# A transformer block on one core: attention scores in two passes, with no transposes

## The chip, the cores and the metric

The kernel runs on one core of one Trainium2 chip. The metric is the time of one execution on the device in microseconds (us); lower is better.

## The reference, cut to what matters

The reference is a block of two branches over 1,024 positions of width 1,024, a gated merge, a feed-forward part, a convolution part and a second feed-forward part. The change is in the first branch's attention: 8 heads, 64 + 32 query and key columns, values of 64 columns, no mask.

```python
def blocked_mla_attention(q_nope, q_rope, k_nope, k_rope, v):
    ...
    scale = 1.0 / math.sqrt(QK_NOPE + QK_ROPE)
    ...
        s = (jnp.einsum('bqhd,bkhd->bhqk', qn_b, k_nope)
             + jnp.einsum('bqhd,bkd->bhqk', qr_b, k_rope))
        p = jax.nn.softmax(s.astype(jnp.float32) * scale, axis=-1)
        return jnp.einsum('bhqk,bkhd->bqhd', p.astype(v.dtype), v)
```

The second branch, which shares the stage with attention, is a linear recurrence over the positions with a state of 64x64 for each of 8 heads (`wkv7_scan`), once forward and once backward; the results of both directions are normalized, gated and added.

## The kernel before

The kernel is written in direct mode: each engine has its own instruction stream, and signals (semaphores) with `wait_ge` order them. Positions lie along the free dimension in most stages; weights come in 139 panels of 1 MB, which ScalarE and VectorE split into a high and a low fp32r part, and big products are sums of three fp32r matmuls.

The stage of the change holds the two recurrences and attention. The recurrence is computed in eight steps (tiles of 128 positions) for each direction; these are "ways" d = 0 and d = 1, and way 1 starts 13 places later. One step of a way is cut into named calls: `cum` (prefix sums of the decays, L1335 to L1338, and ScalarE's exponentials of them, L1483 to L1492), `mul` (VectorE's four multiplications L1550 to L1558), `turn` (16 transposes, L1347, and ScalarE's copies L1501 and L1506 into AR, BT and KT), `scores` (L1358, masked by VectorE at L1563), `PV`, `Nc` (a small block to DRAM and back in another layout as Dn, L1696 and L1700), `row0` to `row3` (VectorE's small forward substitution, L1590 and L1592), `spread` (L1598, and three memsets on GpSimd, L1681), `X`, `Y3` to `X5` (the block inverse, L1375 to L1404), `WU` (L1414), `RG` (L1424, added by VectorE at L1627), `OH` (L1432 to L1447), `S0` and `S1` (the state, L1462 and L1468), and `post1` to `post3` (group norm and gate: VectorE L1648 to L1652, a square on ScalarE at L1533, a power on GpSimd at L1684, four multiplications and additions on VectorE at L1660 to L1670).

`slots()` writes one common order for all engines: in each place stands one call of way 1, one call of way 0 and zero, one or two attention halves, by the table `EACH`, which repeats after 27 places and has 16 attention halves in them. Way calls stand first in a place. Every engine runs through this order and takes its part of each call, so an instruction that waits holds up all that stands behind it on its engine.

Attention is cut into 64 units u, each one head h of a pair k and one block of 128 queries. Queries Qb are stationary and keys Kp stream (L1744), so scores lie with queries on the partitions and 1,024 keys along two PSUM banks, 4 and 5. VectorE takes the negated maximum of each row (L1774), ScalarE the exponential with that as its bias and the row's sum in the same instruction (L1790), VectorE the reciprocal (L1777), ScalarE scales the row (L1795). TensorE transposes P in eight blocks of 128x128 into bank 6 (L1767, four in each half), ScalarE copies them to PT (L1785, L1801), and every second unit TensorE multiplies them by the values Vp into bank 7, two heads beside each other on 64 partitions each (L1755). ScalarE copies four such results to Oh (L1807), and GpSimd's queue stores them. Halves c = 0 and c = 1 of unit u are two attention places. A score product waits for the exponential of the unit before.

## Time and profile before

| | us |
|---|---|
| median of 3 runs | 3265.0 |
| lowest and highest | 3261.01 and 3273.98 |
| the profiled execution, own time | 3276.46 |
| its span | 3274.6 |

The profiled execution is one run; its span is the time from its first to its last instruction. Engines are named PE (TensorE's matmuls), PEld (TensorE's weight loads, beside the matmuls), DVE (VectorE), ACT (ScalarE), POOL (GpSimd) and SP (SyncE, whose queue issues most DMAs). An f32 matmul has two records of each kind, an fp32r one has one. Matmuls overlap, so the sum of their durations is more than the time they take: the chain of work counts overlapping records once. L followed by a number is a line of the kernel.

### The profile page before, as it was taken

To read this page: it belongs to the slowest core of one execution; us is meant where nothing else is said; L and a number is where in the kernel's file an instruction comes from. 1 tells how busy PE (TensorE), PEld (TensorE's weight loads), DVE (VectorE), ACT (ScalarE), POOL (GpSimd) and SP (SyncE) were. 2 spreads that over 40 slices of the span, in tenths; PEclk is the share of its full clock that TensorE was granted. 3 is DMA by queue.
4 is the path that set the end of the run, shared out by engine and by line. 5 is a ranking of instruction groups with operands and counts; after the bars stand their busy time and mean duration, and the time that the engine had idled before them with its cause. 6 is when DMAs were issued, how large, how long until landed. Compare 5 with 4: busy or idle time off the path is not lost.

```text
span 3274.6 us, 54823 instructions
## 1 busy us (share of the span) xinstructions
PE 3152.3 (96%) x23414; PEld 2544.0 (78%) x23414; DVE 2012.7 (61%) x3047; ACT 1067.3 (33%) x1528; POOL 374.1 (11%) x354
## 2 busy tenths in 40 slices
PE   8998998899999998999999999999999999999999
PEld 7787886777777777778888888887746888788887
DVE  6665554466766775545444444469979988755544
ACT  5222334445444443222111111132253333433332
POOL 0222441000000000301000000020000000110000
PEclk9999999799999999999999999999999999999999
DMA  3343665122222223421111111111101222223222
GB/s 148 126 135 99 214 213 186 54 75 81 69 86 75 82 81 116 148 90 52 39 52 52 52 42 49 52 39 52 39 13 52 103 91 103 90 90 126 94 91 76
DMA packets 93537, 288.80 MB, mean 88 GB/s; under 512 B 12400, under 2 KB 38640, under 8 KB 72816
## 3 DMA queue, kind: packets, MB, share of 16 engines
q1 hardware_dynamic: 79104, 233.39, 21.1%
q0 software_dynamic: 14192, 51.91, 4.6%
q8 instruction: 186, 3.05, 0.4%
q14 instruction: 55, 0.45, 0.0%
HBM read 228.64 MB, written 56.62 MB: 87 GB/s over the span
## 4 chain that ended last, share of the span: by engine, by line
PE 82%; DVE 10%; ACT 2%; issue 2%; DMA 2%; POOL 1%; SPq 1%; DVEq 0%; ACTq 0%; POOLq 0%
PE ps L2441 24%; PE ps L307 21%; PE ps L489 7%; PE ps L1744 4%; PE ps L2247 3%; PE ps L2603 2%; PE ps L1755 2%; DVE Yh L2630 2%; PE ps L1767 2%; PE ps L2063 1%; PE ps L1387 1%; PE ps L1404 1%; PE ps L1008 1%; PE ps L1398 1%; DVE wlo L287 1%
## 5 line engine op out<-in xcount | busy, mean ns | idle before, releaser
L2441 PE MATMUL ps<-Hh,whi 128*128 128x512 f32 x1600 | 497.6, 392 | 1.3 <-DVE uA L2562 0.7
L283 ACT ACTIVATE whi<-raw 128x2048 fp32r<-128x2048 f32 x139 | 265.5, 1910 | 522.2 <-PE ps L307 296.1
L287 DVE TENSOR_TENSOR wlo<-raw,whi 128x2048 fp32r<-128x2048 f32 x139 | 321.2, 2311 | 95.0 <-ACT whi L283 94.6
L2441 PEld LDWEIGHTS ps<-Hh,whi 128*128 128x128 f32 x1600 | 300.0, 188 | 70.5 <-issue 5.3
L2441 PE MATMUL ps<-Hh,wlo 128*128 128x512 f32 x800 | 311.4, 389 | 0.0
L307 PE MATMUL ps<-Hhi,wlo 128*128 128x512 f32 x672 | 206.9, 389 | 0.0
L307 PE MATMUL ps<-Hlo,whi 128*128 128x512 f32 x672 | 206.9, 389 | 0.0
L307 PE MATMUL ps<-Hhi,whi 128*128 128x512 f32 x672 | 206.8, 389 | 0.0
L2441 PE MATMUL ps<-aHh,whi 128*128 128x512 f32 x512 | 199.5, 390 | 2.7 <-DVE wlo L287 2.5
L2441 PE MATMUL ps<-aLh,whi 128*128 128x512 f32 x512 | 199.2, 389 | 0.0
L2441 PE MATMUL ps<-aHh,wlo 128*128 128x512 f32 x512 | 199.2, 389 | 0.0
L2809 DVE TENSOR_TENSOR xT<-ps,xT 128x512 f32<-128x512 f32 x256 | 169.2, 687 | 21.3 <-PE ps L2441 21.3
L2441 PEld LDWEIGHTS ps<-Hh,wlo 128*128 128x128 f32 x800 | 150.2, 188 | 31.5
L489 PE MATMUL ps<-Hhi,whi 128*128 128x512 f32 (+1 forms) x512 | 163.8, 401 | 0.0
L2309 DVE TENSOR_TENSOR xT<-ps,xT 128x512 f32<-128x512 f32 x176 | 112.3, 686 | 77.0 <-PE ps L307 76.0
L2630 DVE SCALAR_TENSOR_TENSOR Yh<-uB,vc,Yh 128x512 f32<-128x512 f32 x208 | 157.8, 761 | 3.0
L489 PE MATMUL ps<-Hlo,whi 128*128 128x512 f32 (+1 forms) x512 | 158.9, 392 | 0.0
L489 PE MATMUL ps<-Hhi,wlo 128*128 128x512 f32 (+1 forms) x512 | 158.0, 390 | 0.0
L2795 DVE TENSOR_TENSOR aLh<-rth,aHh 128x512 fp32r<-128x512 f32 x64 | 43.5, 722 | 170.2 <-ACT aHh L2789 170.2
L307 PEld LDWEIGHTS ps<-Hhi,wlo 128*128 128x128 f32 x672 | 126.1, 188 | 26.2
L307 PEld LDWEIGHTS ps<-Hhi,whi 128*128 128x128 f32 x672 | 126.1, 188 | 26.2
L307 PEld LDWEIGHTS ps<-Hlo,whi 128*128 128x128 f32 x672 | 126.1, 188 | 26.2
(389 smaller groups left out, 6181.8 us busy)
## 6 DMA issues: line engine op xcount, KB each, us to landing
raw<-in_panels SPq DMA_DIRECT2D x139, 1024.0 KB, 4.8
rwf<-F POOLq DMA_DIRECT2D x16, 1280.0 KB, 6.6
L<-rwf SPq DMA_DIRECT2D x16, 1024.0 KB, 5.0
L<-rwf SPq DMA_DIRECT2D x64, 256.0 KB, 3.5
gts<-so POOLq DMA_DIRECT2D x16, 512.0 KB, 3.5
gl<-gts SPq DMA_DIRECT2D x32, 256.0 KB, 3.6
rwt<-so POOLq DMA_DIRECT2D x15, 512.0 KB, 2.9
qkd<-XTs POOLq DMA_DIRECT2D x16, 384.0 KB, 4.0
```

The source lines that it names most:

```text
L283: e.activation(whi[i % 2][:, :], raw_of(i)[:, :], AF.Copy).then_inc(*a_hi.up(i))
L287: e.tensor_tensor(wlo[i % 2][:, :], raw_of(i)[:, :], whi[i % 2][:, :].bitcast(F32), OP.subtract).then_inc(*v_lo.up(i))
L307: m = e.matmul(aps[h][0:n1 - n0, :], w[wi][:, kc, n0:n1], mov[mi][:, kc, hs(h)], start=x == 0 and q == 0, stop=x == len(kcs) - 1 and q == 2)
L489: m = e.matmul(aps[h][0:n1 - n0, :], W[wi][:, kc, n0:n1], H2[mi][:, kc, hs(h)], start=kc == 0 and q == 0, stop=kc == 7 and q == 2)
L1744: m = e.matmul(bank[4 + half], Qb[g % 3][:, h, :], Kp[k % 2][:, h, hs(half)], start=True, stop=True)
L1755: m = e.matmul(bank[7][64 * n:64 * n + 64, 128 * (w % 4):128 * (w % 4) + 128], Vp[(w // 8) % 2][:, i, 64 * n:64 * n + 64], PT[:, i, n, :], ...
L1767: m = e.transpose(bank[6][:, 128 * q:128 * (q + 1)], Pb[w % 2][:, 128 * i:128 * (i + 1)], ident)
L2247: m = e.matmul(aps[h], W[wi][:, kc, n0:n0 + 128], H2[mi][:, kc, hs(h)], start=kc == 0 and q == 0, stop=kc == 7 and q == 2)
L2309: e.tensor_tensor(xT[:, n, hs(h)], ring.bank("down", p, n, h), xT[:, n, hs(h)], OP.add).then_inc(*v.up("x", b, n, h))
L2441: m = e.matmul(ap, W[wi][:, kc, n0:n0 + 128], mov[mi][:, kc, :], start=x == 0 and q == 0, stop=x == len(kcs) - 1 and q == 2)
L2630: e.scalar_tensor_tensor(out=to, in0=x, scalar=w, in1=to, op0=OP.mult, op1=OP.add).then_inc(*v_e.up(*key))
L2809: e.tensor_tensor(xT[:, n, hs(h)], ring.bank("x", h, b, n), xT[:, n, hs(h)], OP.add).then_inc(*v_e.up("x", h, b, n))
```

## The change

Attention now runs over eight groups g, each a pair of heads and one half (512) of the queries, and over 128 items in place of 128 halves (`att_items`): for each group eight of the first pass ("max") and eight of the second ("exp"). The places in the common order are as before, and four further ones at the end hold what is left.

First pass: as L1744 before, with queries stationary, but read as fp32r, one record per matmul. VectorE takes the negated maxima into negm. TensorE turns the eight columns of a group into rows, by 64 matmuls in all with one stationary column and the identity streaming ("row"), and ScalarE copies them as a 97th partition under the queries Qr. The keys Kr have a 97th partition of ones, set by two memsets at the start.

Second pass: keys are stationary in blocks of 128 and 512 queries of each head stream, in f32 with 97 contraction rows, so the maximum is already subtracted and scores lie with keys on the partitions. ScalarE's exponential of both heads' 512 columns goes to Pe, which is the streaming operand of PV as it stands, accumulated over the eight key blocks in bank 6 or 7. GpSimd adds the eight Pe of a group into acc (seven additions of 128x1024). At a group's end TensorE multiplies acc by a block of ones (L1789, "sum"), which gives every partition of a head the column's sum; ScalarE copies it to Oh (L1856); VectorE takes the reciprocal of 128x512 (L1831) and multiplies PV by it (L1834) ("out"); GpSimd's queue stores it. The recurrences, the places and the rest of the kernel are unchanged.

`ALSO` says behind which item these extra pieces stand. `PAIR` names for each product in banks 4 and 5 the item or sum before it, and `pair_free` waits until that one has been read: a maximum by VectorE, an exponential or a sum by ScalarE.

```diff
-    Kp = [sb(f"Kp{i}", 8 * i, [96, 2, S]) for i in range(2)]
-    Pb = [sb(f"Pb{i}", 16 + 4 * i, [128, S]) for i in range(2)]
-    PT = sb("PT", 24, [128, 8, 2, 128])
+    Kr = [sb(f"Kr{i}", 8 * i, [97, 2, S], F32R) for i in range(2)]
+    Pe = [sb(f"Pe{i}", 16 + 4 * i, [128, 2, 512]) for i in range(2)]
+    acc = sb("acc", 24, [128, 2, 512])
+    Qr = [sb(f"Qr{i}", (28, 170, 174)[i], [97, 2, 512], F32R) for i in range(3)]
     Vp = [sb(f"Vp{i}", 32 + 4 * i, [128, 8, 128]) for i in range(2)]
-    st_m = sb("st_m", 40, [128, 64])
-    st_s = sb("st_s", 40.25, [128, 64])
-    st_r = sb("st_r", 40.5, [128, 64])
-    Oh = [sb(f"Oh{i}", 170 + 2 * i, [128, 512]) for i in range(2)]
-    Qb = [sb(f"Qb{i}", 174 + i, [96, 2, 128]) for i in range(3)]
+    negm = sb("negm", 40, [128, 64])
+    Oh = sb("Oh", 201.28125, [128, 512])
     oas = dram("oas", [4, 128, S])
-    t_at, v_at, a_at = signals("t_at"), signals("v_at"), signals("a_at")
-    d_kp, d_vp, d_qb, d_oa = landings("d_kp", 2), landings("d_vp", 2), landings("d_qb", 3), landings("d_oa", 2)
+    t_at, v_at, a_at, g_at = signals("t_at"), signals("v_at"), signals("a_at"), signals("g_at")
+    d_kp, d_vp, d_qr, d_oa = landings("d_kp", 2), landings("d_vp", 2), landings("d_qr", 3), landings("d_oa", 1)
...
+    def att_items():
+        made = [("max", 0, j) for j in range(8)]
+        for g in range(7):
+            made += [("max", g + 1, 0)]
+            for j in range(7):
+                made += [("max", g + 1, j + 1), ("exp", g, j)]
+            made += [("exp", g, 7)]
+        return made + [("exp", 7, j) for j in range(8)]
...
+    def also():
+        on = {}
+        for i, (c, g, j) in enumerate(ITEMS):
+            if c == "exp":
+                on.setdefault(i + (2 if g < 7 else 1), []).append(("PV", g, j))
+                on.setdefault(i + 1, []).append(("acc", g, j))
+                if j == 7:
+                    on.setdefault(i + (4 if g < 6 else 3 if g < 7 else 2), []).append(("sum", g, 0))
+                    on.setdefault(i + (5 if g < 6 else 4 if g < 7 else 3), []).append(("out", g, 0))
+            if c == "max" and j == 7:
+                on.setdefault(i + (2 if g else 1), []).append(("row", g, 0))
+        return on
...
+    def before_of():
+        made, last = {}, None
+        for i in range(len(ITEMS) + 4):
+            for key in [key for key in ALSO.get(i, ()) if key[0] == "sum"] + ITEMS[i:i + 1]:
+                made[key], last = last, key
+        return made
...
     def q_sp(e, g):
+        k, qh = g // 2, g % 2
         if g >= 3:
+            e.wait_ge(*t_at.by("B", g - 3, 7))
+        e.dma_start(Qr[g % 3][0:96, :, :].bitcast(F32), qkd[0, :, 2 * k:2 * k + 2, hs(qh)]).then_inc(*d_qr.up(g))
+    def pair_free(e, *key):
+        before = PAIR[key]
+        if before:
+            c, g, j = before
+            e.wait_ge(*(v_at.by("max", g, j) if c == "max" else a_at.by("E", g, j) if c == "exp" else a_at.by("sum", g)))
     def att_pe(e, u, c):
+        i = 2 * u + c
+        for name, g, j in ALSO.get(i, ()):
+            if name == "row":
+                e.wait_ge(*v_at.by("max", g, 7))
+                if g >= 2:
+                    e.wait_ge(*v_at.by("O", g - 2))
+                for h in range(2):
+                    for q in range(4):
+                        m = e.matmul(bank[6 + g % 2][96 - 32 * h:97 - 32 * h, 128 * q:128 * (q + 1)],
+                                     negm[:, 8 * g + 4 * h + q:8 * g + 4 * h + q + 1], ident, start=True, stop=True)
+                m.then_inc(*t_at.up("row", g))
+            if name == "sum":
+                pair_free(e, "sum", g, 0)
+                e.wait_ge(*g_at.by("acc", g, 7))
+                for h in range(2):
+                    m = e.matmul(bank[4][64 * h:64 * h + 64, :], ones[:, 0:64], acc[:, h, :], start=True, stop=True)
+                m.then_inc(*t_at.up("sum", g))
+        if i < len(ITEMS):
+            name, g, j = ITEMS[i]
+            k = g // 2
+            if name == "max":
+                if j == 0:
+                    e.wait_ge(*d_kp.by(k))
+                    e.wait_ge(*d_qr.by(g))
+                pair_free(e, "max", g, j)
+                for half in range(2):
+                    m = e.matmul(bank[4 + half], Qr[g % 3][0:96, j % 2, 128 * (j // 2):128 * (j // 2) + 128],
+                                 Kr[k % 2][0:96, j % 2, hs(half)], start=True, stop=True)
+                m.then_inc(*t_at.up("A", g, j))
+            else:
+                if j == 0:
+                    e.wait_ge(*a_at.by("row", g, 1))
+                    if g < 3 and g != 1:
+                        e.wait_ge(*v_at.by("ones", k))
+                pair_free(e, "exp", g, j)
+                for h in range(2):
+                    m = e.matmul(bank[4 + h], Kr[k % 2][:, h, 128 * j:128 * (j + 1)].bitcast(F32),
+                                 Qr[g % 3][:, h, :].bitcast(F32), start=True, stop=True)
+                m.then_inc(*t_at.up("B", g, j))
+        for name, g, j in ALSO.get(i, ()):
+            if name == "PV":
+                if j == 0 and g % 2 == 0:
+                    e.wait_ge(*d_vp.by(g // 2))
+                e.wait_ge(*a_at.by("E", g, j))
+                for h in range(2):
+                    m = e.matmul(bank[6 + g % 2][64 * h:64 * h + 64, :], Vp[(g // 2) % 2][:, j, 64 * h:64 * h + 64],
+                                 Pe[j % 2][:, h, :], start=j == 0, stop=j == 7)
+                m.then_inc(*t_at.up("PV", g, j))
     def att_dve(e, u, c):
+        i = 2 * u + c
+        if i == 0:
+            for n in range(2):
+                e.memset(Kr[n][96:97, :, :].bitcast(F32), 1.0).then_inc(*v_at.up("ones", n))
+        for name, g, j in ALSO.get(i, ()):
+            if name == "out":
+                e.wait_ge(*a_at.by("sum", g))
+                e.reciprocal(Oh[:, :], Oh[:, :]).then_inc(*v_at.up("rec", g))
+                e.wait_ge(*v_at.by("rec", g))
+                e.wait_ge(*t_at.by("PV", g, 7))
+                e.tensor_tensor(Oh[:, :], bank[6 + g % 2], Oh[:, :], OP.mult).then_inc(*v_at.up("O", g))
+        if i < len(ITEMS):
+            name, g, j = ITEMS[i]
+            if name == "max":
+                n = 8 * g + 4 * (j % 2) + j // 2
+                e.wait_ge(*t_at.by("A", g, j))
+                e.tensor_reduce(negm[:, n:n + 1], ps[:, 2048:3072], AX, OP.max, negate=True).then_inc(*v_at.up("max", g, j))
     def att_act(e, u, c):
+        i = 2 * u + c
+        for name, g, j in ALSO.get(i, ()):
+            if name == "row":
+                e.wait_ge(*t_at.by("row", g))
+                if g >= 3:
+                    e.wait_ge(*d_qr.by(g))
+                for h in range(2):
+                    e.activation(Qr[g % 3][96:97, h, :], bank[6 + g % 2][96 - 32 * h:97 - 32 * h, :],
+                                 AF.Copy).then_inc(*a_at.up("row", g, h))
+            if name == "sum":
+                e.wait_ge(*t_at.by("sum", g))
+                if g:
+                    e.wait_ge(*d_oa.by(g - 1))
+                e.activation(Oh[:, :], bank[4], AF.Copy).then_inc(*a_at.up("sum", g))
+        if i < len(ITEMS):
+            name, g, j = ITEMS[i]
+            if name == "exp":
+                e.wait_ge(*t_at.by("B", g, j))
+                n = 8 * g + j - 2
+                if n >= 0:
+                    e.wait_ge(*t_at.by("PV", n // 8, n % 8))
+                    e.wait_ge(*g_at.by("acc", n // 8, max(1, n % 8)))
+                e.activation(Pe[j % 2][:, :, :], ps[:, 2048:3072].rearrange("p (h t) -> p h t", h=2),
+                             AF.Exp).then_inc(*a_at.up("E", g, j))
     def att_pool(e, u, c):
+        i = 2 * u + c
+        for name, g, j in ALSO.get(i, ()):
+            if name == "acc" and j:
+                e.wait_ge(*a_at.by("E", g, j))
+                if j == 1 and g:
+                    e.wait_ge(*t_at.by("sum", g - 1))
+                if j > 1:
+                    e.wait_ge(*g_at.by("acc", g, j - 1))
+                e.tensor_tensor(acc[:, :, :], Pe[0][:, :, :] if j == 1 else acc[:, :, :], Pe[j % 2][:, :, :],
+                                OP.add).then_inc(*g_at.up("acc", g, j))
+            if name == "out":
+                e.wait_ge(*v_at.by("O", g))
+                e.dma_start(oas[g // 2, :, hs(g % 2)], Oh[:, :]).then_inc(*d_oa.up(g))
     def att_sp(e, u, c):
+        i = 2 * u + c - 8
+        if i >= 0 and i % 16 == 5:
+            g = i // 16 + 2
+            if 3 <= g < 8:
+                q_sp(e, g)
+            if g in (4, 6):
+                kv_sp(e, g // 2)
...
```

TensorE, once in a period, where X5 of way 1 (L1404) is followed by WU (L1414), RG (L1424) and OH (L1432). Before:

```order
L1404 MATMUL ps<-XT_162,E_155 64x32 x16
L1767 MATMUL ps<-cc,Pb_173 128x128 x4
L1414 MATMUL ps<-AP_157,XT_162 64x128 x16
L1744 MATMUL ps<-Kp_172,Qb_185 128x512 x2
L1767 MATMUL ps<-cc,Pb_174 128x128 x4
L1424 MATMUL ps<-SC_156,WU_154 64x128 x16
L1432 MATMUL ps<-L_114,SC_156 64x64 x16
```

After:

```order
L1404 MATMUL ps<-XT_162,E_155 64x32 x16
L1789 MATMUL ps<-acc,cc 64x512 x2
L1800 MATMUL ps<-Kr_171,Qr_177 128x512 x2
L1414 MATMUL ps<-AP_157,XT_162 64x128 x16
L1810 MATMUL ps<-Qr_176,Kr_172 128x512 x2
L1819 MATMUL ps<-Pe_173,Vp_180 64x512 x2
L1424 MATMUL ps<-SC_156,WU_154 64x128 x16
L1432 MATMUL ps<-L_114,SC_156 64x64 x16
```

The sums' product and a first-pass product have come ahead of WU, and the second-pass product with its PV stands between WU and RG.

VectorE at the same place: L1652 ends post1 of way 0, L1622 copies WU, L1590 and L1592 are row0. Before:

```order
L1652 TENSOR_TENSOR Os_137<-Os_137,sc_140 128x512
L1777 RECIPROCAL st_r<-st_s 128x1
L1622 COPY WU_154<-ps 128x512
L1590 TENSOR_TENSOR pr_143<-Xc_142,Dn_121 128x8x2
L1592 TENSOR_REDUCE Xc_142<-pr_143 128x8
L1590 TENSOR_TENSOR pr_143<-Xc_142,Dn_121 128x8x3
L1592 TENSOR_REDUCE Xc_142<-pr_143 128x8
L1774 TENSOR_REDUCE st_m<-ps 128x1
L1627 TENSOR_TENSOR RG_161<-ps,AR_158 128x512 x2
```

After:

```order
L1652 TENSOR_TENSOR Os_137<-Os_137,sc_140 128x512
L1840 TENSOR_REDUCE negm<-ps 128x1
L1622 COPY WU_154<-ps 128x512
L1590 TENSOR_TENSOR pr_143<-Xc_142,Dn_121 128x8x2
L1592 TENSOR_REDUCE Xc_142<-pr_143 128x8
L1590 TENSOR_TENSOR pr_143<-Xc_142,Dn_121 128x8x3
L1592 TENSOR_REDUCE Xc_142<-pr_143 128x8
L1831 RECIPROCAL Oh<-Oh 128x512
L1834 TENSOR_TENSOR Oh<-ps,Oh 128x512
L1627 TENSOR_TENSOR RG_161<-ps,AR_158 128x512 x2
```

The maxima have moved ahead of the WU copy, the small reciprocal is gone, and the reciprocal of 128x512 with its product stands ahead of the RG additions (L1627).

GpSimd, one period: L1684 is rstd's power in post2, L1687 the store of post3, L1681 the memsets of spread. Before:

```order
L1684 TENSOR_TENSOR sc_167<-sc_167,cc 128x8
L1687 DMA obs<-Os_164 128x512
L1681 MEMSET Y_151 128x512
L1681 MEMSET Y_150 128x512
L1681 MEMSET E_155 128x512
L1684 TENSOR_TENSOR sc_140<-sc_140,cc 128x8
L1687 DMA obs<-Os_137 128x512
L1681 MEMSET Y_124 128x512
L1681 MEMSET Y_123 128x512
L1681 MEMSET E_128 128x512
L1813 DMA oas<-Oh_181 128x512
```

After:

```order
L1684 TENSOR_TENSOR sc_140<-sc_140,cc 128x8
L1877 TENSOR_TENSOR acc<-Pe_173,Pe_174 128x1024
L1687 DMA obs<-Os_137 128x512
L1681 MEMSET Y_124 128x512
L1681 MEMSET Y_123 128x512
L1681 MEMSET E_128 128x512
L1877 TENSOR_TENSOR acc<-acc,Pe_173 128x1024
L1877 TENSOR_TENSOR acc<-acc,Pe_174 128x1024
L1877 TENSOR_TENSOR acc<-acc,Pe_173 128x1024
L1684 TENSOR_TENSOR sc_167<-sc_167,cc 128x8
L1877 TENSOR_TENSOR acc<-acc,Pe_174 128x1024
L1687 DMA obs<-Os_164 128x512
```

Seven additions (L1877) stand among them in each group, two of them right behind a power.

## Rows read from the trace of the kernel before

**Rows 1.** The page, engines: busy us, share of the span, instructions.

```profile
PE 3152.3 (96%) x23414; PEld 2544.0 (78%) x23414; DVE 2012.7 (61%) x3047; ACT 1067.3 (33%) x1528; POOL 374.1 (11%) x354
```

**Rows 2.** Windows: start:end, length, busy us of each engine, clock, DMA share, GB/s.

```profile
527.00:591.00 64.00, 50.39 (x385) 31.25 (x386) 26.26 (x54) 36.00 (x57) 2.00 (x4) 0.84 0.26 86
591.00:703.30 112.30, 103.25 (x1878) 86.88 (x1876) 64.01 (x140) 47.31 (x83) 5.70 (x9) 0.88 0.22 67
875.90:960.00 84.10, 79.43 (x1563) 63.86 (x1561) 58.42 (x129) 41.84 (x73) 7.95 (x11) 1.00 0.30 89
1044.30:1131.90 87.60, 82.97 (x1563) 65.68 (x1561) 59.78 (x131) 42.02 (x73) 7.95 (x11) 0.96 0.24 77
```

**Rows 3.** TensorE's waits, 525 to 1220: us, times, longest.

```profile
PE ps L1432 <- DVE RG L1627: 15.9, 14, 5.1
PE ps L1358 <- ACT KT L1506: 9.2, 8, 1.7
```

**Rows 4.** Chain of work, one period: start us, us, what.

```profile
810.83 0.23 PE ps L1335
...
824.91 0.59 PE ps L1767 x4
...
828.46 1.90 PE ps L1755 x32
...
839.50 1.91 PE ps L1744 x4
```

**Rows 5.** Timeline of TensorE in that period: start us, us, instructions [idle before <-releaser].

```profile
835.66 1.09 PE L1404 MATMUL ps<-XT,E 64*64 64x32 f32 x29
...
837.53 1.96 PE L1414 MATMUL ps<-AP,XT 64*64 64x128 f32 x32 [0.20 <-DVE XT L1618]
...
843.90 1.05 PE L1432 MATMUL ps<-L,SC 64*64 64x64 f32 x29 [0.91 <-DVE RG L1627]
```

**Rows 6.** Timeline of VectorE, same stretch.

```profile
838.31 0.69 DVE L1652 TENSOR_TENSOR Os<-Os,sc 128x512 f32<-128x512 f32 x1
...
839.54 0.69 DVE L1622 COPY WU<-ps 128x512 f32<-128x512 f32 x1 [0.47 <-PE ps L1414]
...
843.07 1.29 DVE L1627 TENSOR_TENSOR RG<-ps,AR 128x512 f32<-128x512 f32 x2 [0.32 <-PE ps L1424]
```

**Rows 7.** Timeline of ScalarE, same stretch.

```profile
839.04 0.63 ACT L1533 ACTIVATE E<-Os 128x512 f32<-128x512 f32 x1 [6.36 <-DVE Os L1652]
```

**Rows 8.** Groups by line: count | busy us, mean ns | idle before; the last two outside the stage.

```profile
L1774 DVE TENSOR_REDUCE st_m<-ps 128x1 f32<-128x1024 f32 x64 | 78.3, 1224 | 55.8 <-PE ps L1744 54.8
...
L1785 ACT ACTIVATE PT<-ps 128x512 f32<-128x512 f32 x64 | 38.3, 598 | 182.6 <-PE ps L1767 182.6
...
L1777 DVE RECIPROCAL st_r<-st_s 128x1 f32<-128x1 f32 x64 | 10.1, 158 | 12.3 <-ACT Pb L1790 12.1
...
L2510 DVE RECIPROCAL rsh<-rsh 128x512 f32<-128x512 f32 x6 | 20.1, 3348 | 4.1 <-ACT rsh L2496 4.1
...
L2389 POOL TENSOR_TENSOR cv<-cv,rs 128x1024 f32<-128x1024 f32 x22 | 52.7, 2393 | 713.5 <-ACT cv L2376 713.5
```

**Rows 9.** Timelines, 2795 to 2804; then single lines: ns min/median/max, first to last start.

```profile
2795.26 8.10 DVE L2662 TENSOR_TENSOR Yh<-Yh,rsh 128x512 f32<-128x512 f32 x6
...
2797.78 6.74 POOL L2464 TENSOR_TENSOR sgt<-sgt,uB 128x512 f32<-128x512 f32 x4
...
L2662 DVE TENSOR_TENSOR Yh<-Yh,rsh x16: 684/689/1786, 2420.8 to 2801.6; 128x512 f32<-128x512 f32 x16
...
L2175 POOL TENSOR_TENSOR mix<-mix,gl x12: 1287/1769/3342, 1317.9 to 1355.2; 128x512 f32<-128x512 f32 x12
...
L2139 DVE TENSOR_TENSOR gl<-ps,gl x16: 675/682/692, 1317.1 to 1367.3; 128x512 f32<-128x512 f32 x16
```

**Rows 10.** Chain of work in the front.

```profile
559.91 1.43 DMA nbs<-Nc
...
568.14 0.20 DVE pr L1590
```

93 lines of the change are left out of this document (8 added, 85 removed).

## The prediction

> **What bounds the kernel now.** I read the page first, then the windows over the stage that the change touches, then groups of instructions, waits and the timeline of one period. TensorE is busy for 96% of the span [rows 1], so what counts is TensorE's order and what it waits for. The touched stage runs from 527 to about 1218 us. There two recurrences, forward and backward, run side by side, and attention fills the gaps between their steps. Each of their steps repeats after 27 places in the order with 16 attention places among them, that is 8 units of one head and 128 queries. In the windows such a period takes 84.1 to 87.6 us; TensorE is busy for 79.4 to 83.0 us of it, VectorE for 58.4 to 59.8 us, ScalarE for 42 us and GpSimd for 8 us [rows 2]. TensorE is thus the bound, but with 4.5 to 5.5 us of idle time per period, and VectorE is only a little behind. TensorE's waits are short and nearly all for the recurrences: in the whole stage 15.9 us for VectorE's RG adds and 9.2 us for ScalarE's KT copies, the two largest [rows 3]. The front, 527 to 591 us, is different: TensorE is busy for only 50.4 of 64 us, at a mean granted clock of 0.84 [rows 2].
>
> **The change part by part.** TensorE's prices come from the chain, where overlapping records are counted once [rows 4]: a score product (two 512-column f32 matmuls) 1.91 us; four transposes 0.59 us; a PV group of 16 matmuls at 128 columns 1.90 us; an fp32r matmul of 512 columns 0.23 us.
>
> *TensorE work.* Away go 128 groups of transposes, 75.5 us. The second scores have 97 contraction rows in place of 96 and as many columns, 64 x 1.91 us, as before. PV streams 64 x 512 columns for each half, as many as 32 x 8 x 128; the 2,048 columns of one group would take 3.8 us at the scores' 0.955 us for 512, and the row has 1.90, so the two 64-wide halves overlap. I take 0.95 us for each pair, the old total; one after the other they would cost 61 us more, but the halves are the same parts of the array as before. Added are the maxima, 64 x 2 x 0.23 = 29.4 us, the negated maxima turned into a row, 64 small matmuls at the 0.15 us of a transpose, 9.5 us, and the sums over partitions, 8 x 0.95 = 7.6 us. Net: -29 us. Where it lies matters. The first 17 places hold 13 maxima, a row, four second products and three PV pairs, 17.7 us, for nine scores, 16 groups of transposes and four PV groups, 34.2 us: 16.5 us less, but not bound by TensorE (below). A steady period loses 16 x 0.59 - 8 x 0.46 - 1.2 - 0.95 = 3.6 us, over 6.4 periods 23 us. The rest of the -29 us is +10 us in the last 12 places, which hold nine second products for six units. On the path: **-13 us**.
>
> *The sums' wait.* The sums' product takes the score banks, so the maxima product behind it on TensorE waits for ScalarE's copy of the sums. In ScalarE's order that copy stands behind the recurrence's square (L1533), which waits for VectorE's subtraction of the mean. In the period shown TensorE has done X5's matmuls at 836.75 us [rows 5]; VectorE ends the subtraction at 839.00 [rows 6]; the square lets the next instruction start at 839.6 and lets the copy, 0.6 us, end at 840.2 [rows 7]. TensorE would have done the sums at 837.7 and wait until 840.3: 2.6 us, and the WU matmuls, which started at 837.53, stand behind it. Six groups stand in this place, the seventh costs the bare copy, 0.75 us, the eighth falls into the Dn wait: **+17 us**.
>
> *Reciprocals.* VectorE loses 64 reciprocals of 0.16 us and gains eight of 128x512, at 3.35 us by the row of that shape [rows 8], and eight products of 0.69 us, as L1652 [rows 6]. VectorE runs them between the WU copy and the RG adds, for which TensorE already waits. From the end of WU: copy 0.8 with its signal, row0's four instructions 0.8 (from 840.15 to 840.99, to be seen between the rows of L1622 and L1627), reciprocal and product 4.04, first RG add 0.85 with its signal [rows 6], so the next matmul can start after 6.5 us. TensorE's own cover is scores 1.91, PV 0.95 and RG 1.08 = 3.94 us; it waits 2.5 us where it now waits 0.91 [rows 5]. That is 1.6 us in each of six periods: **+10 us**. If the sums' wait has let VectorE get ahead, nothing; if there is no cover, 4 x 8 = 32 us.
>
> *Adds on GpSimd.* 56 adds of 128x1024 take 2.39 us each by L2389 [rows 8], 134 us on an engine with 8 us per period. ScalarE needs them only two exponentials later, so they aren't late themselves. What they do to VectorE is the larger term. In the late stretch VectorE's multiplications L2662, with both inputs in SBUF, have a median of 0.69 us, but six of them take 8.10 us beside GpSimd's adds, and the longest 1.79: the two alternate [rows 9]. L2139, with one input in PSUM, stays at 675 to 692 ns in a stretch where GpSimd's L2175 run between the same times [rows 9]. In the changed order GpSimd's add stands right behind rstd's power (L1684) twice a period, and VectorE's four L1660 to L1670 wait for just that power: GpSimd goes on into the add, VectorE is held for up to 2.4 us, and the step's multiplications (L1550 to L1558) and transposes stand behind. A third add follows the memsets (L1681) into L1550 to L1558, a fourth meets the Nc and bm instructions; three meet PSUM work only. I charge three holds of 2.4 us at half, since TensorE has a maxima or PV group as cover, and 0.5 for the fourth: 4 us per period, 6.5 periods: **+26 us**. Bounds: 0, if every hold is covered, and 56 x 2.39 = 134 us. The Trainium skill, SBUF — State Buffer, "Who interferes with whom", gives this as an exclusive lock on a shared port pair, which takes in a VectorE instruction with two SBUF inputs and leaves out reductions and those with one. That the maxima's reductions are left out no row here shows at their length; were they held too, all seven adds would count, and the sum would be about 20 us higher, by the page it stays.
>
> *ScalarE.* It loses per unit two PT copies of 0.60 us [rows 8] and the scaling of P. It isn't the bound. But its Exp no longer waits for a maximum in the same place, and the KT and E copies behind it come earlier: of the 9.2 us that TensorE waited for KT, eight times [rows 3], I give back **-6 us**, and the range has 0 and -9.
>
> *Maxima.* The same 64 reductions of 1.22 us; each product now waits for the consumer of the one before. In most places 1.9 us or more of the recurrences' matmuls lie between; where one Y4 (1.1 us) does, up to 0.5 us is left, once a period. I take 0, and 3 us for the range.
>
> *Front.* Before, the step's own chain rules: Nc to DRAM at 559.91, eight loads issued one after another, first row at 568.14 [rows 10]. The change puts eight maxima ahead, each product waiting for the reduction before, and two memsets of one partition x 2048 ahead of them; by the 1.22 us of a reduction over 1,024 columns [rows 8] up to 2.4 us each, and I take that. Walking it through, Nc gets to DRAM 2 us later: **+3 us**, bounds -16 (the work lost, were TensorE the bound) and +8. The granted clock there has a mean of 0.84, at 1.2 GHz for a third of the time, and from 591 to 703 us one of 0.88, which is 27 us at 1.2 GHz [rows 2]. With fewer matmuls in the front that level may last longer; as long again after 591 would cost 13 us. The Trainium skill, TensorE: Matmul & The Clock Gate, Part 1, has it that the slow level is the default which activity lifts; by that rule the sum would be 13 us higher, by the rows of before it stays.
>
> *DMA.* Queries come as 8 loads instead of 32, with the same bytes and issued a group ahead; keys and values as before. I take nothing, since no wait for a load of them is among TensorE's largest [rows 3].
>
> **Sum.** -13 + 17 + 10 + 26 - 6 + 3 = +37 us. The profiled execution took 3276.5 us (span 3274.6), above the median of 3265.0 and all three timed runs, so its own time would become 3313 us; what is timed I expect at 3265 + 37, rounded: **3300 us**.
>
> **Rivals.** (1) *Work decides.* The adds' holds and the reciprocals fall into time in which VectorE waits for TensorE anyway; VectorE has 25 us of such time a period, which speaks for it; TensorE's idle time of only 5 us, set by these very VectorE results, speaks against. With the sums' wait halved: -13 - 6 + 8 = -11, and with the front's 16 us, -27: about 3240 us. It decides when fewer than one hold per period reaches TensorE. (2) *A draw.* The sums' wait and the reciprocals count, the adds' holds don't: +11, 3276 us, within noise. (3) *VectorE becomes the bound.* Its busy 58.5 us a period grow by 2.8 and by up to 7 x 2.39 = 16.7 of holds to 78; with waits for TensorE it can't be packed so tightly, and a period grows by 10 us: 3335 us. It needs the lock in most adds. (4) *The change doesn't do what it says*: were the fp32r maxima to run at the f32 price, 64 x (1.91 - 0.46) = 93 us more, 3390 us; L1335 and L1336, both fp32r, speak against.
>
> **Numbers.** Forecast 0.45, (1) 0.15, (2) 0.20, (3) 0.17, (4) 0.03. The range takes in the draw and most of (1) and (3): 3245 to 3350 us. A measurement here can tell about 0.5%, 16 us: faster than 3249 us 0.13, within 0.22, slower than 3281 us 0.65.
>
> **What would show it.** A period of 88 to 91 us with TensorE busy for 76 to 79; TensorE's wait before the maxima product behind L1789 of 2.6 us, released by the copy L1856; one of 2.5 us before L1432, once a period; L1660, L1550 and their like at 1.5 to 3 us beside L1877. If those stay at 0.69 us, the term of 26 us is wrong; if they are long and TensorE's idle time isn't, my charge of half is. If the front ends before 580 us, I misread its bound.

## The result and the profile after

The changed kernel took a median of 3341.9 us (3340.2 to 3351.4, 4 runs) beside 3268.5 us (4 runs) of the kernel before: a ratio of 1.023 [1.020, 1.026], 73 us slower where I had forecast 35. The direction is right and the time lies in the range; the size of the loss is twice the forecast. The profiled execution took 3351.4 us (span 3349.6), 75 us more than that of before.

The page, its engines row and the row of the granted clock (tenths, 40 slices of the span), answer to [rows 1]:

```profile
PE 3183.5 (95%) x22422; PEld 2496.3 (75%) x22422; DVE 2072.2 (62%) x3001; ACT 939.3 (28%) x1288; POOL 508.3 (15%) x410
...
PEclk9999997889899988999999999999999999999999
```

TensorE has 992 matmuls fewer and is busy 31 us longer: its clock must be looked at. The windows (columns as in [rows 2]) of the whole stage, from 527 us to the start of the last WU, and of its front alone, which ends where the first WU starts; the kernel before:

```profile
527.00:1270.90 743.90, 681.63 (x12304) 543.18 (x12304) 473.75 (x1024) 347.38 (x594) 61.90 (x87) 0.95 0.25 79
527.00:618.20 91.20, 77.59 (x777) 55.81 (x777) 36.16 (x74) 43.59 (x70) 2.00 (x4) 0.78 0.23 76
```

and the changed kernel, with two of its periods:

```profile
527.00:1351.40 824.40, 717.56 (x11310) 498.83 (x11310) 534.07 (x978) 219.64 (x354) 195.94 (x143) 0.89 0.22 71
527.00:619.10 92.10, 68.04 (x618) 41.82 (x618) 44.76 (x69) 20.15 (x31) 11.39 (x8) 0.68 0.23 81
...
725.50:815.40 89.90, 80.93 (x1437) 56.56 (x1436) 63.89 (x122) 25.97 (x43) 23.94 (x18) 0.98 0.28 83
815.40:913.50 98.10, 89.56 (x1437) 62.98 (x1436) 64.24 (x122) 25.98 (x43) 25.62 (x19) 0.88 0.20 63
```

The stage is 80.5 us longer, and these rows split it. TensorE's idle time (length less busy) goes from 62.3 to 106.8 us, +44.5. The clock, a mean of 0.95 before and 0.89 after, spends 79 and 188 us at 1.2 GHz; half of what TensorE is busy in those stretches, taken one by one from the records, is 35 and 78 us, +43. What is left, its work as if at 2.4 GHz, is 647 and 639 us, -7. The front took 92.1 us for 91.2, but it isn't the same front: idle time 24.1 for 13.6 us, clock 21.7 for 19.2, work 46 for 58. Behind the front the stage is 79.6 us longer: idle time +34 (48.7 to 82.8), clock +41 (16 to 57), work +5 (588 to 593). The two periods do the same work; one took 89.9 us at a clock of 0.98 and the other 98.1 at 0.88. Each kernel below is split in this manner.

TensorE's waits from 525 to 1290 us (columns as in [rows 3]):

```profile
PE ps L1432 <- DVE RG L1627: 24.1, 14, 5.7
PE ps L1800 <- ACT Oh L1856: 14.5, 6, 2.4
PE ps L1347 <- DVE SC L1557: 9.8, 6, 1.9
PE ps L1800 <- DVE negm L1840: 8.3, 5, 2.3
PE ps L1347 <- DVE AP L1550: 8.1, 8, 2.1
PE ps L1810 <- DVE negm L1840: 6.6, 4, 3.1
...
PE ps L1358 <- ACT KT L1506: 1.1, 5, 0.2
```

L1800 is the maxima product, L1810 the second score product. The two lines that wait for negm, 14.9 us, stand with the same numbers in the view of the front, 527 to 619.1 us; from there to 1351.4 us TensorE waits for no maximum. The kernel before waits 16.8 us at L1432 in the same window. And the timeline of TensorE around one group's end, the place of [rows 5]:

```profile
856.06 1.08 PE L1789 MATMUL ps<-acc,cc 128*64 128x512 f32 x4
859.58 0.73 PE L1800 MATMUL ps<-Kr,Qr 96*128 96x512 f32 x2 [2.45 <-ACT Oh L1856]
860.25 3.57 PE L1414 MATMUL ps<-AP,XT 64*64 64x128 f32 x32
863.75 2.00 PE L1810 MATMUL ps<-Qr,Kr 97*128 97x512 f32 x4
...
870.16 1.44 PE L1432 MATMUL ps<-L,SC 64*64 64x64 f32 x29 [2.37 <-DVE RG L1627]
```

The two waits stand where the prediction put them, with 2.45 us for its 2.6 and 2.37 for its 2.5. What it doesn't have is the row between: the WU products L1414, 1.96 us in [rows 5], take 3.57 us right behind the wait, that is at 1.2 GHz, and the ones of L1432 behind the second wait 1.44 for 1.05.

Groups of after (count | busy us, mean ns | idle before):

```profile
L1877 POOL TENSOR_TENSOR acc<-acc,Pe 128x1024 f32<-128x1024 f32 x48 | 115.6, 2408 | 196.1 <-ACT Pe L1865 195.8
L1557 DVE TENSOR_TENSOR SC<-L,E 128x512 f32<-128x512 f32 x16 | 23.9, 1494 | 0.0
L1831 DVE RECIPROCAL Oh<-Oh 128x512 f32<-128x512 f32 x7 | 23.5, 3352 | 0.2
```

and L1557's of before:

```profile
L1557 DVE TENSOR_TENSOR SC<-L,E 128x512 f32<-128x512 f32 x16 | 11.0, 685 | 0.0
```

GpSimd's adds and the reciprocals cost what the prediction took for one; L1557, two SBUF inputs beside an add, is more than twice as long in the mean.

And the prices of TensorE's new pieces, from the chain of work of after (as [rows 4]; L1782 is the row of one group, L1819 a PV pair):

```profile
745.04 1.41 PE ps L1782 x16
...
751.19 0.66 PE ps L1800 x2
751.85 1.01 PE ps L1819 x4
```

### The profile page after: what moved, and what is told of

Its sections match the earlier page's. It is cut to its first block, busy times and chain, and to the rows that moved or that the text cites. A ratio compares the mean times of both kernels' runs of the same rounds, so it can differ in the third digit from the quotient of the medians.

```text
span 3349.6 us, 52396 instructions
## 1 busy us (share of the span) xinstructions
PE 3183.5 (95%) x22422; PEld 2496.3 (75%) x22422; DVE 2072.2 (62%) x3001; ACT 939.3 (28%) x1288; POOL 508.3 (15%) x410
## 4 chain that ended last, share of the span: by engine, by line
PE 78%; DVE 14%; issue 3%; POOL 2%; DMA 1%; ACT 1%; SPq 0%; DVEq 0%; ACTq 0%; POOLq 0%
PE ps L2512 24%; PE ps L307 21%; PE ps L489 7%; PE ps L1810 3%; PE ps L2318 2%; PE ps L2674 2%; DVE Yh L2701 2%; PE ps L2134 1%; PE ps L1819 1%; PE ps L1404 1%; PE ps L1387 1%; PE ps L1800 1%; PE ps L1008 1%; PE ps L1398 1%; PE ps L1414 1%
## 5 line engine op out<-in xcount | busy, mean ns | idle before, releaser
L2460 POOL TENSOR_TENSOR cv<-cv,rs 128x1024 f32<-128x1024 f32 x22 | 52.7, 2393 | 710.0 <-ACT cv L2447 710.0
L1810 PE MATMUL ps<-Qr,Kr 97*128 97x512 f32 x256 | 139.8, 672 | 7.3 <-DVE negm L1840 6.6
```

The source lines that it names most:

```text
L1810: m = e.matmul(bank[4 + h], Kr[k % 2][:, h, 128 * j:128 * (j + 1)].bitcast(F32), Qr[g % 3][:, h, :].bitcast(F32), start=True, stop=True)
L2460: e.tensor_tensor(cv, cv, rs2, OP.mult).then_inc(*g_ff.up(ch))
```

## The experiments

Kernels whose names begin with a are the changed one with an edit, those with b the kernel before with one. The table is their result. The ratio is to the kernel before as it was timed in the same round (medians of 3268.3 to 3270.6 us); "clock" is the median of the executions' mean granted clocks. Idle, clock us and work are the split above, of the one profiled execution, for the stage. Within one kernel the time follows the clock: over 127 executions of these kernels, each taken against the mean of its kernel, 0.001 of mean clock is 2.4 us, with a correlation of -0.94. By this price alone the fall of the medians from 0.985 to 0.970 is 35 of the 73 us.

| kernel | median us | ratio | clock | idle | clock us | work |
|---|---|---|---|---|---|---|
| before | 3268.5 | 1 | 0.985 | 62 | 35 | 647 |
| after | 3341.9 | 1.023 [1.020, 1.026] | 0.970 | 107 | 78 | 639 |
| a1_no_adds | 3323.0 | 1.018 [1.015, 1.020] | 0.970 | 88 | 66 | 638 |
| a2_fill | 3344.9 | 1.023 [1.022, 1.025] | 0.977 | 84 | 48 | 685 |
| a3_sum_early | 3339.4 | 1.021 [1.016, 1.026] | 0.971 | 99 | 90 | 639 |
| a4_out_late | 3371.1 | 1.032 [1.029, 1.034] | 0.963 | 112 | 95 | 637 |
| a5_no_norm | 3307.8 | 1.012 [1.011, 1.014] | 0.974 | 90 | 56 | 633 |
| a6_no_norm_adds | 3291.9 | 1.007 [1.004, 1.010] | 0.969 | 67 | 69 | 628 |
| a7_dense_no_norm_adds | 3278.3 | 1.002 [1.001, 1.004] | 0.978 | 65 | 34 | 639 |
| a8_dense | 3360.8 | 1.027 [1.024, 1.029] | 0.967 | 105 | 73 | 646 |
| a9_all_f32 | 3412.2 | 1.043 [1.041, 1.045] | 0.974 | 97 | 59 | 722 |
| a10_short_max | 3340.3 | 1.021 [1.018, 1.024] | 0.969 | 98 | 70 | 640 |
| a11_no_max_norm_adds | 3230.6 | 0.988 [0.986, 0.990] | 0.984 | 38 | 35 | 627 |
| a12_no_max | 3318.1 | 1.015 [1.014, 1.017] | 0.974 | 88 | 60 | 641 |
| b1_before_adds | 3293.9 | 1.008 [1.005, 1.010] | 0.983 | 75 | 42 | 648 |
| b3_before_waits | 3320.2 | 1.016 [1.014, 1.018] | 0.980 | 99 | 48 | 647 |
| b4_before_light | 3261.3 | 0.998 [0.997, 0.999] | 0.986 | 63 | 22 | 642 |
| b5_before_all_light | 3223.1 | 0.986 [0.984, 0.988] | 0.983 | 77 | 39 | 579 |

### The adds, left out and put in

```diff
-            if name == "acc" and j:
+            if name == "acc" and j == 7:
...
-                e.tensor_tensor(acc[:, :, :], Pe[0][:, :, :] if j == 1 else acc[:, :, :], Pe[j % 2][:, :, :],
-                                OP.add).then_inc(*g_at.up("acc", g, j))
+                e.memset(acc[:, :, 0:256], 1.0).then_inc(*g_at.up("acc", g, j))
+                e.memset(acc[:, :, 256:512], 1.0).then_inc(*g_at.up("acc'", g, j))
```

> The changed kernel without GpSimd's 56 adds of 128x1024; acc is filled by two memsets per group instead, so the softmax sums are left out. Theory A (the adds hold VectorE's two-SBUF instructions, and the longer waits that follow also bring TensorE down to 1.2 GHz more often): about 45 us less than the changed kernel's 3342, near 3297, with TensorE's mean granted clock in the stage up from about 0.90 to 0.95 or more, and L1557 and L1660 back at 0.69 us. Theory B (the adds cost their charge of 26 us and nothing else): 3316, clock as before. Theory C (the adds hide, the missing 40 us lie in the maxima's waits alone): within 10 us of 3342.

Into the kernel before, at the same places, went two adds of 128x512 of a tile of their own for each:

```diff
+        if n in ADDED:
+            e.wait_ge(*a_at.by("E", min(u, 63)))
...
+            for k in range(2):
+                e.tensor_tensor(xtra[:, :], xtra[:, :], xtra[:, :], OP.add).then_inc(*g_x.up("x", n, k))
```

> The kernel before with 112 GpSimd adds of 128x512 on a tile of their own, two in each place where the changed kernel has one add of 128x1024, each pair behind the exponential of its place. This prices the holds alone, with all else as before. By the prediction's charge 26 us: 3294. Theory A (holds bring the clock down too): 35 to 45 us, 3305 to 3313, with a stage clock under 0.95. Theory C: under 10 us.

Left out, 19 us go; put in, 24 us come (3293.9 beside 3269.7 of the kernel before, timed with it). In a1_no_adds L1557 is back to

```profile
L1557 DVE TENSOR_TENSOR SC<-L,E 128x512 f32<-128x512 f32 x16 | 11.0, 685 | 0.0
```

and idle time falls by 19 us. So the adds act through VectorE's instructions, as charged, at 19 to 24 us for my 26. The low clock stays (0.970), and the 45 us of Theory A don't come.

### Sums one place earlier, reciprocals one place later

```diff
-                    on.setdefault(i + (4 if g < 6 else 3 if g < 7 else 2), []).append(("sum", g, 0))
+                    on.setdefault(i + (3 if g < 7 else 2), []).append(("sum", g, 0))
```

> The sums' product one item earlier for groups 0 to 5, where no square stands ahead of its copy in ScalarE's order. If the wait of 2.4 us, six times, is on the path as the prediction has it: 10 to 14 us less, about 3330, and TensorE's wait for L1856 down from 14.5 us to 5 us. If that wait only moves to another place: within 3 us of 3342.

The time stayed (3339.4 for 3341.9 us). The wait for L1856 fell from 14.5 to 5.4 us, L1810's for maxima rose from 6.6 to 10.8, and the four executions spread from 3320 us at a clock of 0.978 to 3357 at 0.963: the wait can be moved, but what the move is worth is lost in the clock.

```diff
-                    on.setdefault(i + (5 if g < 6 else 4 if g < 7 else 3), []).append(("out", g, 0))
+                    on.setdefault(i + (6 if g < 6 else 4 if g < 7 else 3), []).append(("out", g, 0))
```

> The changed kernel with the reciprocals and the products with them one place later (i + 6 in place of i + 5, g < 6), behind another piece of the scan. Nothing is left out. By the prediction's term of the reciprocals (10 us in six periods, the wait of L1432 for VectorE 2.37 us where it was 0.91) their wait gets shorter by some 8 to 10 us in all and the time falls by that: 3332 to 3335 us beside 3342. By the theory that TensorE's granted clock falls behind each new wait, the clock comes back with it, and the time falls by 15 to 25 us. By the rival that VectorE has no spare time in the period anyway, the wait moves to the next line that needs VectorE and the time stays at 3342.

29 us slower than the changed kernel, which no theory had. TensorE's waits in a4_out_late:

```profile
PE ps L1810 <- DVE negm L1840: 23.6, 10, 3.1
PE ps L1432 <- DVE RG L1627: 17.5, 14, 5.9
```

The reciprocal left RG's way (24.1 to 17.5 us) and came into that of a maximum that a score product waits for (6.6 to 23.6). One place later VectorE's 4 us are seen as well, and cost more; other places weren't tried.

### Without the division, then without the adds too

```diff
-                for h in range(2):
-                    m = e.matmul(bank[4][64 * h:64 * h + 64, :], ones[:, 0:64], acc[:, h, :], start=True, stop=True)
...
-                e.reciprocal(Oh[:, :], Oh[:, :]).then_inc(*v_at.up("rec", g))
...
+                e.tensor_copy(Oh[:, :], bank[6 + g % 2]).then_inc(*v_at.up("O", g))
```

> The changed kernel with the division by the sums left out: no ones product, no copy of it, no reciprocal; the output is unnormalised. The POOL adds stay. TensorE loses 8 products of 1.07 us, the wait of 2.45 us behind each of them (14.5 us in all) and the reciprocal's part of L1432's wait (24.1 to some 16 us). Theory A (the clock falls behind the new waits): idle 20 us shorter, work 9 us less, and 30 to 50 us of clock back: 3265 to 3285 us, mean clock 0.98 or above. Theory B (the clock falls because TensorE's work is less dense or of another kind, whatever it waits for): the clock stays at 0.968 to 0.972 and the time is 3342 - 9 - 22 = 3305 to 3315 us.

> As a5_no_norm, with the POOL adds left out too (output unnormalised): what is left of the change is the score products, the exponentials without transposes, PV and the row of maxima. The adds cost 19 us in a1_no_adds. Theory A: 3245 to 3265 us, at the kernel before or under it, clock 0.98 or above. Theory B: 3286 to 3296 us at a clock of 0.97.

a5_no_norm is 34 us faster than the changed kernel; its profiled execution is 43 us under the other: idle 17, clock 23, work 7 in the split. The time is Theory B's (3305 to 3315 us), the clock of 0.974 lies between the two. L1432 waits 14.5 us for RG here, less than in the kernel before. a6_no_norm_adds is another 16 us faster, with the time and the clock of Theory B: its idle time is nearly that of the kernel before, yet its clock is 0.969. Behind the front it even waits less than the kernel before, 43 us for 49, and loses 50 us by the clock for 16. Two windows of it:

```profile
859.00:871.80 12.80, 11.83 (x242) 8.53 (x240) 8.30 (x18) 3.62 (x6) 1.45 (x3) 1.00 0.42 146
871.80:888.90 17.10, 16.57 (x213) 12.14 (x214) 8.13 (x20) 1.65 (x2) 0.00 (x0) 0.50 0.07 18
```

and what TensorE does there:

```profile
869.24 1.12 PE L1398 MATMUL ps<-Y,XT 64*64 64x32 f32 x32 [0.53 <-DVE Y L1608]
870.19 1.10 PE L1404 MATMUL ps<-XT,Y 64*64 64x32 f32 x32
871.22 0.73 PE L1794 MATMUL ps<-Kr,Qr 96*128 96x512 f32 x2
871.89 0.80 PE L1462 MATMUL ps<-St,RG 64*64 64x64 f32 x10
```

The clock falls for 17.1 us, with no wait over 0.53 us ahead and TensorE busy for 11.8 of 12.8 us. It does so in five periods running, each time at this place: behind solve products of 64x32 and a one-pass maxima product (L1794), where the kernel before has four transposes. This costs 8.3 us a period, half of the 16.57 that TensorE is busy in it, and is a second kind of fall beside the one behind a wait.

### Is it the light work?

```diff
+                    if j == 5 and 2 <= g <= 6:
+                        a, b = a.bitcast(F32), b.bitcast(F32)
```

> a6_no_norm_adds with five of the 64 one-pass maxima products (j = 5 of g = 2 to 6) run as plain float32 products, four times as long (some 1.25 us more for each). In the trace of a6_no_norm_adds the granted clock falls once a period for 17.1 us, and TensorE's products turn slow each time right behind this product, which stands between the solve's products of 64x32 and L1462, with waits of 0.5 us only beside it. Nothing else changes; the output is unnormalised as in a6_no_norm_adds. Theory C (the cheap product in that place makes TensorE's work there too light to hold 2.4 GHz): the five long stretches are gone, 5 x 8.5 us come back and 5 x 1.25 go: 3292 - 36 = 3256 us, clock 0.979 or above. Theory A (only waits bring it down): nothing changes but the 6 us, 3298 us at 0.969.

> The changed kernel with the same five maxima products as plain float32. Nothing is left out. Its trace has three stretches of 17.1 us at the low clock behind that place (718, 906 and 1189 us) and many of 3.4 and 6.8 us behind the waits. Theory C: the three go (26 us back, 6 us of work more): 3318 to 3325 us, and the short ones stay. Theory A: 3348 us.

In the kernel before, the score product of that place was cut (b4), then all of them (b5):

```diff
+            wide = 192 if u % 8 == 5 and 16 <= u < 56 else 512
-                m = e.matmul(bank[4 + half], Qb[g % 3][:, h, :], Kp[k % 2][:, h, hs(half)], start=True, stop=True)
+                m = e.matmul(bank[4 + half][:, 0:wide], Qb[g % 3][:, h, :],
+                             Kp[k % 2][:, h, 512 * half:512 * half + wide], start=True, stop=True)
```

> The kernel before with five of its 64 score products (the ones in that same place of the period) cut to 192 of 512 columns in each half, so that they take about as long as the changed kernel's one-pass product: some 0.75 us in place of 1.98. The scores of those five blocks are not all computed. Work falls by 6 us. Theory C: TensorE's clock now falls there as in the changed kernel, up to 5 x 8.5 us: 3268 - 6 + 20 to 43 = 3282 to 3305 us at a clock of 0.97 to 0.977. Theory A: 3262 us at 0.984.

> The kernel before with all 64 score products cut to 192 of 512 columns in each half, about as long as the changed kernel's one-pass products; the scores are not all computed. TensorE's work falls by 64 x 1.25 = 80 us, no wait is added. Theory C: the clock falls as in the changed kernel, to 0.965 to 0.975, and gives back 30 to 60 us: 3220 to 3250 us. Theory A: the clock stays at 0.98 or above and the time falls by 60 to 80 us less what VectorE and ScalarE then bound: 3190 to 3210 us.

And all 64 maxima products of the changed kernel as float32:

> The changed kernel with all 64 maxima products as plain float32 in place of the one-pass kind; nothing else. TensorE gets 64 x 1.25 = 80 us more work, so that its score work is as long as before the change plus the second pass. Theory C (the one-pass products make TensorE's work too light to hold the clock): the clock goes back to 0.98 or above, 40 us come back: 3342 + 80 - 40 = 3382 us. Theory A (the waits bring it down, whatever the products are): the clock stays at 0.967 to 0.972 and the time is 3415 to 3425 us; less, by up to 15 us, if the longer products hide VectorE's reductions.

In a7 four of the five long falls went, and 14 of the 36 us expected came; one fall of 20.5 us is left (and 10 us of what its profiled execution gained lie in the front, where nothing was edited). Its ten executions go from 3268 us at 0.982 (the profiled one) to 3295 at 0.971. In a8 the three long falls of the changed kernel (from 706.8, 894.5 and 1177.8 us of the span; the expectation names them 11 us later) went too, and one of 20.5 us came in a period that had none:

```profile
1077.78 3.61 PE L1803 MATMUL ps<-Kr,Qr 96*128 96x512 f32 x4
```

That is the float32 product itself, put in for the light one, at half speed from its start: the fall begins at 1078.0 us, behind the same solve products. The one left in a7, at 934.1 us, begins in the float32 product too (3.69 us). So a fall comes at this place with the heavy product as well as with the light one. The place is what the traces share: between 650 and 1230 us the kernels of the changed order have 29 falls of 17.1 us or more, one to five in each but a9_all_f32, which has none, and all 29 begin at the maxima product behind a wait of 0.53 us and the solve products of 64x32 (L1398, L1404). The kernel before and the four made from it have no fall of that length there, though they have the solve products and the short wait too. What in the new order ahead of that place makes the difference was not tested.

a8 got 19 us slower in the median, 7 of it work and, by the price above, some 10 the clock, which is 0.004 lower. b4 gained 8 us with the clock 0.002 higher, b5 47 us with the clock 0.002 lower (3270.6 of before beside it; work 68 us less, idle time 14 more). a9 cost 70 us for some 80 us of work, with the clock up by 0.003, where Theory C had 0.98 and 40 us back. So a long fall doesn't need the light product, though changing it moves the falls; on the side of before, lighter work left the clock nearly alone.

### Is it the waits?

> The kernel before with seven reciprocals of 128x512 of a tile of its own on VectorE, at the places where the changed kernel has them, and seven waits of TensorE for ScalarE's copy of its last transposes, at the places where the changed kernel waits for the copy of the sums. Nothing of the computation is changed; the same two waits are put into a kernel with the old, denser work. The waits by themselves: 7 of 1 to 2.5 us for ScalarE and 7 of 1.5 more before L1432: 18 to 28 us, so 3286 to 3296 us. Theory A adds the clock falling behind them, as in the changed kernel: 20 to 45 us more, 3310 to 3340 us, and a mean clock of 0.970 to 0.975 in place of 0.983. Theory B: the clock stays at 0.983 and the time at 3286 to 3296.

```diff
+        if 2 * u + c in LONG2:
+            e.wait_ge(*a_at.by("PT", w))
...
+        if n in LONG:
+            e.wait_ge(*v_x.by(LONG.index(n)))
+            e.reciprocal(xtra[:, :], xtra[:, :]).then_inc(*v_x.up(LONG.index(n) + 1))
```

```profile
PE ps L1414 <- ACT PT L1813: 30.1, 7, 6.7
PE ps L1432 <- DVE RG L1627: 26.0, 15, 5.1
```

```profile
856.81 3.68 PE L1414 MATMUL ps<-AP,XT 64*64 64x128 f32 x32 [3.91 <-ACT PT L1813]
```

52 us slower than the kernel before. The waits by themselves were longer than I had put them, 37 us more idle time in the stage (30.1 new at L1414, and 26.0 for 16.8 at L1432); the clock falls for 6.8 us at six of the seven inserted ones, as the row shows at L1414, and takes 13 us more. So waits like the changed kernel's, in the old work, bring a loss of clock of a third of their own length; in the changed kernel it is as long as the added idle time itself. The Trainium skill, TensorE: Matmul & The Clock Gate, "HAM oscillation — how this bites in real kernels", describes a kernel that waits once per iteration and has the clock down once per iteration. The trace of b3_before_waits agrees, with one fall of 6.8 us in each of six periods; the long falls of a6_no_norm_adds, with no long wait ahead, don't follow from it.

Last, the maxima: reductions over half the scores, and then none (the row of maxima a zero, the exponent scaled by 0.1):

```diff
-                e.tensor_reduce(negm[:, n:n + 1], ps[:, 2048:3072], AX, OP.max, negate=True)
+                e.tensor_reduce(negm[:, n:n + 1], ps[:, 2048:2560], AX, OP.max, negate=True)
```

> The changed kernel with each maximum taken over 512 of the 1024 scores (and the exponent scaled by 0.1, so that no value overflows; same instructions): the maxima and the exponentials are not the reference's. VectorE is freed of 64 x some 0.57 us = 37 us. Theory V (VectorE's load makes the maxima waits of 15 us and a part of L1432's 24 us): the waits for negm fall from 15 to under 6 us, L1432's by some 6 us, and the time by 15 to 30 us with the clock that comes back: 3312 to 3327 us. Rival (the order of the banks makes the waits: each maxima product stands right behind another pair's user): they shrink only by the 0.57 us each, 9 x 0.57 = 5 us, and the time by 5 to 10 us, 3332 to 3337 us.

> a6_no_norm_adds with the 64 reductions to maxima left out too (the row of maxima is zero, the exponent is scaled by 0.1; output not the reference's). TensorE does the same products as in a6_no_norm_adds, but no maxima or score product waits for VectorE: 19.3 us of waits go (L1794 8.3, L1804 11.0). Theory A (waits lower the clock): the five stretches of 17.1 us go with them: 3292 - 19 - 41 = 3232 us, clock 0.98 or above. Theory D (something else in the new TensorE work lowers it): 3270 to 3275 us at a clock of 0.966 to 0.972.

> The changed kernel with only the reductions to maxima left out (row of maxima zero, exponent scaled by 0.1): adds, sums, reciprocals and all of TensorE's products stay. The waits for maxima (14.9 us) go and some 10 us of L1432's 24 and of L1347's 18. Theory A: idle 25 to 35 us less and as much of the clock back in proportion (50 us of clock went with 45 of idle): 3342 - 55 to 65 = 3277 to 3287 us. Theory D: 3307 to 3317 us at a clock of 0.968.

a10 gained 2 us for 34 us of VectorE (689 for 1222 ns, 64 times): the maxima's waits, all in the front, went from 14.9 to 10.5 us, and RG's stayed at 25. They shrank by the half microsecond that each reduction lost, nine times, which fits the rival: TensorE waits for the reduction of the product just before it, in the shared banks 4 and 5, and not for a busy VectorE. It doesn't cover all of them: the longest, 3.1 us, stayed. a11 took 61 us off a6_no_norm_adds, and 38 off the kernel before: idle 29 less, clock 33 less, with the same products on TensorE. Theory A's 3232 us came out to 2 us, but not by its account: two of the five long falls are still there, and most of the gain is in the front, which ends 38 us earlier, with 21 us of the idle time and 15 of the clock:

```profile
527.00:579.50 52.50, 49.00 (x622) 33.38 (x622) 24.64 (x51) 16.29 (x27) 1.73 (x3) 0.93 0.34 113
```

Behind the front a11 waits 34 us and loses 32 by the clock, the kernel before 49 and 16. a12, the same in the full kernel, gave 24 us only, and neither theory's number. In the profiled executions the stage is 35 us shorter, 22.5 of it in the front and 12.6 behind. The maxima's waits are gone, L1432 and the sums' copy stay as they were, and L1347 waits for AP instead:

```profile
PE ps L1432 <- DVE RG L1627: 23.7, 15, 4.3
PE ps L1802 <- ACT Oh L1857: 14.7, 6, 2.5
PE ps L1347 <- DVE AP L1550: 12.8, 11, 2.0
```

### Filling TensorE's time

```diff
+                for _ in range(FILLS):
+                    e.matmul(ap, trir[:, 0, :], trir[:, :, :].rearrange("p a b -> p (a b)"), start=True, stop=True)
```

> The changed kernel with matmuls added that compute nothing that is used: two fp32r ones of 512 columns ahead of each of the four waits in a turn, and eight behind the sums' product, where TensorE waits for ScalarE's copy. They are 27 us and 14 us of work at 0.21 us each, of which 18 us and 14 us lie in waits that TensorE has there now. Theory A (the clock at 1.2 GHz for 100 us more than before is worth 30 to 40 us): the stage's mean clock rises to 0.95 or more and the time falls by 15 us or more in spite of the work. Rival (the low clock falls into waits and costs nothing): 5 to 15 us slower.

The clock went up to 0.977 and gave 30 us back, idle time fell by 23, and the added work took 46: the same time in the median (3344.9 for 3341.9 us), between the two expectations. A part of the clock's loss can be bought back, but here not for less than it costs.

## Why the prediction came out too low

**The step that failed is the last one before the sum: the clock.** I kept it at its level of before and named 13 us, in the front, as what would come if it didn't. In the profiled pair it took 43 us of the stage's 80, by the price over all executions 35 of the 73: the front 2 or 3 us, the steady part up to 1143 us 25, the end 15. The rejected term expected more in the front and right behind it; some 11 us did come there, up to 725 us, but most of it in one fall of 17.1 us at 706.8. The rest comes from places all along the stage: 22 stretches at 1.2 GHz in place of nine, among them short ones behind the new waits and three of 17.1 us. Where I charged TensorE a wait, its products behind it turned slow as well.

**TensorE's work: the second miss, and a size.** I had -29 us in all, 13 of it behind the front. The split says -7: -12 in the front and +5 behind it. The maxima product, priced at 0.46 us as twice a 0.23 of L1335 in the chain, takes 0.66, which makes 13 us over 64; a PV pair takes 1.01 us for 0.95 (4 us), the row 1.41 for 1.2. PV's halves do overlap, as taken.

**The sums' wait: right.** 2.45 us for 2.6, six times, 14.5 us for 17 (the terms named add up to 16.4), released by the copy.

**The reciprocals: right in mechanism and size.** 2.37 us for 2.5 at L1432; in all 24.1 us for 16.8, and 25.0 to the end of the stage: +8 for +10. Without them, in a5_no_norm, it is 14.5. One place later they cost 29 us more (a4_out_late).

**Adds: right.** 19 us left out and 24 put in, for 26; of the long ones L1660 was called by name and L1557 as one of L1550 to L1558, while L1550 itself hardly grew. My charge of half the holds was close: the stage's VectorE instructions with two SBUF inputs are 32 us longer in sum.

**Maxima: right behind the front.** I took 0 there, and TensorE waits for no maximum behind 619 us. All 14.9 us of these waits lie in the front.

**Front: the sum right, the bound only in part.** Nc goes to DRAM at 562.96 us for 559.91, 3 us later where I had 2, and the front ends one us later for three (92.1 for 91.2 us). But that is 10 us more of idle time and 2 of clock against 12 of work: I had named the waits for the reductions without pricing them, and that they and the lost work cancel is luck. The Nc round doesn't bound this front: without the maxima's reductions it takes 69.6 us (a12_no_max), without adds, sums and division too 52.

**ScalarE's KT: right**, -8.1 us for -6.

Behind the front my idle terms (17 + 10 + 26 - 6) were 47 us and the trace has 34; the work was -13 and is +5; the clock was 0 and is 41. The first two errors nearly cancel, so what is missing from the forecast looks like one term. A period was to be 88 to 91 us with TensorE busy 76 to 79; 89.9 with 80.9 is one at a clock of 0.98, 98.1 with 89.6 one at 0.88.

**What stays open** is why the changed kernel loses so much more clock per wait than the old one with waits like them (43 us for 44 of idle time, against 13 for 37). Waits are part of it, as b3 shows. They aren't all of it: behind the front, a6 and a11 wait less than the kernel before (43 and 34 us for 49) and lose more by the clock (50 and 32 us for 16), with long falls in stretches without any wait over 0.53 us. That a11's clock is back at the level of before is the front's doing (3 us lost for 19). Light products are not enough by themselves (b4, b5), and a heavy one in that place doesn't prevent a long fall (a7, a8), though a9_all_f32, which has no light maxima product anywhere, has no long fall there. The long falls come at one place of the new order, but in which periods, and whether a fall lasts 3.4 or 17.1 us, changes with shifts of a few us. None of these kernels settles the rule.

No kernel that computes the reference beat the one before. a11 shows what this arrangement takes with maxima, sums and division left out: 3231 us, 38 us below the old kernel; they cost 111. The front alone gives that much (52 us for 91); behind it a11's stage is only 5 us shorter, which is less than two executions of one kernel differ.
